# A limit of four expert gathers in flight, kept by GpSimd's waits

## The reference, cut to what matters

```
def body(xc):
    u = jnp.take(expert_u, xc["idx"], axis=0)
    vv = jnp.take(expert_v, xc["idx"], axis=0)
    a = jax.nn.gelu(jnp.einsum("td,thkd->thk", xc["h"], u))
    return jnp.einsum("thk,thkd->td", xc["g"] * a, vv)
```

## Time and profile before

| | |
|---|---|
| runs of the kernel | 2684.39, 2685.98, 2688.24 us; median 2685.98 |
| the profiled execution | 2693.67 us, its span 2692.1 us |
| POOL busy | 1053.5 us (39%) |
| gathers | 1024: 512 of v, 512 of u |
| read from HBM | 772.35 MB, 287 GB/s over the span |

### The profile page before, as it was taken

How to read it: one execution, slowest core, us unless ns; L and a number is a source line. 1 busy time by engine, 2 the same in 40 slices (tenths; PEclk the granted TensorE clock), 3 DMA queues, 4 the chain that set the end, 5 groups by cost and what they waited for, 6 DMA issues and landing times. The chain is left out here.

```text
span 2692.1 us, 24931 instructions
## 1 busy us (share of the span) xinstructions
PE 2157.3 (80%) x8403; PEld 1327.3 (49%) x8403; DVE 1635.7 (61%) x3138; ACT 755.3 (28%) x1537; POOL 1053.5 (39%) x1121
## 2 busy tenths in 40 slices
PE   6789989999799878777767666799788867777775
PEld 5578847788597564322222222587554322222221
DVE  6578845688656565646564754565564765566554
ACT  4444444544355121211111101354112111101110
POOL 0010010011002046666666666020356666666664
PEclk9899989999899989998999899899899889999988
DMA  7178822488644488999999999834579999999997
GB/s 253 48 266 299 318 83 102 165 321 314 230 167 147 154 315 328 360 370 371 367 365 384 350 375 372 298 132 172 217 282 372 361 377 361 360 386 366 356 370 279
DMA packets 244425, 774.81 MB, mean 288 GB/s; under 512 B 20361, under 2 KB 24873, under 8 KB 244322
## 3 DMA queue, kind: packets, MB, share of 16 engines
q0 software_dynamic: 160512, 587.27, 57.8%
q1 hardware_dynamic: 83810, 186.25, 19.4%
HBM read 772.35 MB, written 1.10 MB: 287 GB/s over the span
## 5 line engine op out<-in xcount | busy, mean ns | idle before, releaser
L2648 PE MATMUL experts_fourth<-experts_v_slot,experts_diagonal 128*128 128x512 f32 x960 | 478.5, 629 | 211.2 <-DMA experts_v_slot<-in_expert_v_dram,experts_at 114.2
L2648 PE MATMUL experts_first<-experts_v_slot,experts_diagonal 128*128 128x512 f32 x1024 | 505.1, 642 | 153.1 <-issue 81.4
L2283 POOL DMA_INDIRECT experts_v_slot<-in_expert_v_dram,experts_at x512 | 485.0, 947 | 355.2 <-issue 135.7
L2648 PEld LDWEIGHTS experts_fourth<-experts_v_slot,experts_diagonal 128*128 128x128 f32 x960 | 171.4, 196 | 518.4 <-issue 477.2
L2648 PEld LDWEIGHTS experts_first<-experts_v_slot,experts_diagonal 128*128 128x128 f32 x1024 | 200.2, 204 | 442.9 <-issue 417.9
L2278 POOL DMA_INDIRECT ring<-in_expert_u_dram,experts_at x368 | 346.9, 943 | 143.1 <-issue 105.8
L2422 DVE CUSTOM_DVE_ANT_0 ring<-ring,experts_second 128x1024 f32<-128x1024 f32 x192 | 230.1, 1219 | 204.7 <-DMA ring<-in_expert_u_dram,experts_at 189.1
L2422 DVE CUSTOM_DVE_ANT_0 ring<-ring,experts_third 128x1024 f32<-128x1024 f32 x176 | 207.7, 1218 | 97.9 <-DMA ring<-in_expert_u_dram,experts_at 93.3
L538 POOL DMA_DIRECT2D mlp_ada_half<-in_w_ada_dram x48 | 36.2, 755 | 531.8 <-DVE csum L659 308.2
L2532 ACT ACTIVATE experts_dots<-experts_dots 128x16 f32<-128x16 f32 x32 | 6.9, 215 | 731.0 <-issue 413.9
L179 DVE TENSOR_TENSOR mix_lo<-ring,mix_hi 128x1024 fp32r<-128x1024 f32 x96 | 132.1, 1383 | 126.6 <-ACT mix_hi L2017 126.5
(11 more groups left out here) (407 smaller groups left out, 3987.1 us busy)
## 6 DMA issues: line engine op xcount, KB each, us to landing
mlp_ada_half<-in_w_ada_dram POOLq DMA_DIRECT2D x48, 1024.0 KB, 6.7
ring<-in_w_in_dram SPq DMA_DIRECT2D x20, 2048.0 KB, 8.3
ring<-in_mlp_w_in_dram SPq DMA_DIRECT2D x16, 2048.0 KB, 10.4
ring<-in_mlp_w_out_dram SPq DMA_DIRECT2D x16, 2048.0 KB
ring<-in_w_query_dram SPq DMA_DIRECT2D x8, 2048.0 KB, 8.1
ring<-in_gla_w_in_dram SPq DMA_DIRECT2D x6, 2048.0 KB, 8.2
ring<-in_w_out_dram SPq DMA_DIRECT2D x4, 2048.0 KB, 7.9
experts_v_slot<-in_expert_v_dram,experts_at POOLq DMA_INDIRECT x512
```

The lines of the kernel that those rows point to most:

```text
L2283: pool.indirect_dma_start(v_slot[:, j % VS, :], None, rows_v, bass.IndirectOffsetOnAxis(ap=at[:, n, j:j + 1], axis=0)).then_inc(v_in[j % V ...
L2648: mm = pe.matmul(y[n // PH][:, b, :], diagonal[n % 2][:, j, :], v_slot[:, j % VS, b * HALF:(b + 1) * HALF], start=n % PH == 0 and j == 0, ...
```

## The change

GpSimd gets more waits in its loop; nothing else is changed. Before a v gather it waits until the v gather two before has landed, before a u gather until the u gather two before has landed. As the two kinds alternate, that is the fourth gather ahead of it. In unit 15, which has v gathers alone, the fourth ahead is v (n, j - 4) for j of 4 or more, and one of the last two u or v gathers of the loop before for j under 4. The prologue and the first two gathers of each kind in unit 1 have no such wait.

```
+                def v_landed(n, j):
+                    pool.wait_ge(v_in[j % VS], v_arrived(n, j))
+
+                def u_landed(n, j):
+                    pool.wait_ge(u_in[j], 16 * n + 16)
...
                 for n in range(1, UNITS):
                     if n < LAST:
                         pool.wait_ge(at_ready, n + 2)
                     for j in range(TOPK):
+                        if n == LAST and j >= 4:
+                            v_landed(n, j - 4)
+                        elif n == LAST and j % 2:
+                            u_landed(n, TOPK - 2 + j // 2)
+                        elif n == LAST:
+                            v_landed(n - 1, TOPK - 2 + j // 2)
+                        elif j >= 2:
+                            v_landed(n, j - 2)
+                        elif n > 1:
+                            v_landed(n - 1, TOPK - 2 + j)
...
                         if n < LAST:
 
                             pool.wait_ge(dots_done, TOPK * n + j + 1)
+                            if j >= 2:
+                                u_landed(n + 1, j - 2)
+                            elif n > 1:
+                                u_landed(n, TOPK - 2 + j)
                             gather_u(n + 1, j)
```

## The result

| | before | after |
|---|---|---|
| runs, median (lowest to highest) | 2687.11 us (2684.39 to 2690.14, 4 runs) | 2859.11 us (2854.76 to 2864.37, 4 runs) |
| ratio | | 1.0641, 95% interval 1.0616 to 1.0665 |
| profiled execution, its span | 2693.67 us, 2692.1 us | 2856.28 us, 2854.7 us |

What follows compares the result with a forecast made beforehand. The experts stages were taken as bound by the gather pace, 1.43 us: POOL's 1.24 us plus late-signal pauses. At 1.50 us, pauses gone, 459 gathers a layer add 32.3 and 30.6 us to 2685.98 us: 2749 us, range 2645 to 2840 us.

Steps and rivals of the forecast that it cites:

- What bounds the kernel now: Experts stages: a gather each 1.43 us, from POOL's 1.24 us plus pauses, as dense transfers make signals between engines late.
- Four bind nearly always: Dense stretches had 5.4 to 6.3 gathers in flight, so a limit of four would bind nearly always.
- The latency with three ahead, 5.87 us: Mean issue-to-use time of the fourth gather of three bursts (5.39, 6.41, 5.80 us); a quarter of it is 1.47 us.
- The gather of 4.27 us: First gather of a burst, 1021.14 to 1025.41, taken as the latency of half a megabyte alone.
- The pace of 1.50 us: Experts stages: one gather each 1.50 us with four in flight, bounds 1.35 to 1.60 us, 62.9 us more over both layers.
- The second reading, 349 GB/s: DMA rate in a burst's first 8 us, with about four in flight; at 524288 bytes a gather it gives 1.50 us.
- The upper bound of 1.60 us: Slowest pace allowed with four in flight: a quarter of the slowest fourth gather's 6.41 us.
- Pauses gone: POOL's pauses ahead of v gathers, 86 and 88 us a layer, taken as 0 us at the slower pace.
- A met wait at nothing: Each of the 460 waits added per layer costs 0 us if already met; at worst 0.30 us.
- The faster rival: The limit cures late signals in the experts stages: landing at 5.39 us, pace 1.35 us, 2611 us; chance 0.22.
- pauses stay on top: Rival: POOL still loses 86 and 88 us beside the new waits, 2923 us; above 2822 us had chance 0.12.
- What would show it: Signs: landing waits of 0.5 us or so, near 350 GB/s, DMA share under 0.95, stretches of 680 to 700 us, rare pauses.

Runs made afterwards that it cites:

- e7b: Kernel before, without a limit, each gather from unit 1 on reading 128 half rows instead of whole ones: 2689.8 us, ratio 0.998.
- e4: Kernel before plus a limit of eight gathers in flight, each landing wait carried by the gather instruction: 2710.6 us, 1.006 of the kernel before.
- e1: Limit of four as in the change, but the gather itself carries the u landing wait: 2817.7 us, 1.045 of the kernel before.
- e8b: Kernel before, without a limit, ACT signalling its diagonals to PE once for four of them: 2697.8 us, ratio 1.002.
- e9: Kernel before, without a limit, each gather from unit 1 on reading 64 whole rows instead of 128: 2459.0 us, ratio 0.970.
- e18: Kernel before with gathers of 64 whole rows instead of 128 from unit 1 on, run again: 2460.0 us, ratio 0.971.
- e13: Kernel before, unchanged, profiled on a chip where it has no pauses: 2535.1 us, ratio 1.000.

## Why the prediction was right and wrong

- **What bounds the kernel now:** partly wrong. Pauses from late signals are there, but the reason given, that transfers are this dense, fell with e7b.
- **Four bind nearly always:** right; four were in flight (the gather itself counted) at 849 of 880 gathers looked at in the profile after.
- **The latency with three ahead, 5.87 us:** right. It was 5.66 and 5.71 us to the landing and 5.74 and 5.79 us to the use. The gather of 4.27 us, which the prediction takes for a lone one, had company for its first microsecond: the one issued at 1017.24 landed at 1022.19.
- **The pace of 1.50 us: this is the step that failed.** "Reaction of the waiting engine included (POOL will react too)" put POOL's reaction inside the latency, at DVE's size of under 0.1 us. It is 0.76 us and comes on top: (5.69 + 0.76) / 4 = 1.61 us, where 1.608 was measured. Of the 99.5 us by which the stretches exceed 2 x 688.5 us, the reaction is 918 x 0.76 / 4 = 174 us, less 918 x (6.00 - 5.69) / 4 = 71 us by which a latency of 5.69 us is below four times 1.50: together 103 us, within 4 us of it. (Only the u gathers wait for POOL's 0.76 us, but a v gather follows each of them, so the pair moves with it.) The second reading, 349 GB/s, agreed with the first by accident: that window was not limited to four. The upper bound of 1.60 us lacked the reaction too.
- **Pauses gone:** right in the main. Steps of over 3.5 us from one issue to the next fell from 20 and 19 to 5 and 6, and DVE's waits in `choose` for its own signals are gone. But since the pace is above 1.43 us, their 174 us bought nothing.
- **A met wait at nothing:** nearly; in e4 0.016 us if the whole difference is theirs, which would be 15 us for 920.
- **The faster rival** needed a latency under 5.72 us. Measured to the landing it was 5.69 us, to the use 5.74 and 5.79 us, so it stood on the edge, far from the 5.39 us that the rival's 2611 us need; and the reaction is missing from it too. That pauses stay on top (2923 us) fell.
- **What would show it:** landing waits, a share under 0.95 and rare pauses came; stretches of 680 to 700 us and 350 GB/s did not.

## What to carry to other kernels

A limit of K transfers in flight sets a pace of (landing latency under that load + reaction of the issuing engine) / K; work it out with both terms before adding one, and choose K so that the pace of the limit stays below the pace that the kernel has without it. A wait added for a landing should be the one that the DMA instruction carries. A DMA share of 0.97 does not prove that bytes bound the kernel: halving them costs one run. An experiment on a pause that only some chips show needs the kernel before measured on the same chip, and is worth nothing where that has no pauses.

## What the hardware showed that was not expected

- GpSimd begins a gather 0.26 us after the landing that the gather's own wait is for, 0.76 us after it where the wait is an instruction of its own.
- The same kernel took 2687 to 2696 us on the chips of the change and of e1 to e8b, and 2533 to 2536 us on those of e9 to e18. On the former, a signal was seen up to 15.5 us late while gathers go out each 1.24 us, and with half the bytes DVE was still held for 9.6 us by its own (e7b). In e13 no wait of that kind is left, and up to 15 gathers are in flight, landing after 14.9 us at 407 GB/s. No run shows one chip with both times, so this may be a state of a chip and not its kind. The cause of the late signals stays open; a trace with late signals also lacks most records of landing signals (6777 of 19089).
- A 512 KB gather lands after 5.27 us at a pace of 1.86 us, 5.6 at 1.66, 5.9 at 1.57 and 6.04 at 1.44. The Trainium skill (DMA: Bandwidth & Descriptors, "Latency and other measured facts") has latency grow with the load on HBM, and this agrees; its size is only in these runs.
